# One layer of a decoder, DeltaNet branch and 32 experts: the projections from unsplit float32 in place of high and low parts

## The chip, the cores and the metric

The kernel runs on one core of a Trainium2 chip. The metric is the device time of one execution in microseconds (us), median over runs. The core has TensorE (PE in the profile, with its weight loads shown apart as PEld), VectorE (DVE), ScalarE (ACT), GpSimd (POOL), SyncE (SP, which issues most transfers here) and 16 DMA engines.

## The reference, cut to what matters

What is computed is a chain of blocks over 256 tokens of width 1024, all in float32: attention with its input and output projections, a convolutional feed-forward block, a block with a DeltaNet branch and a stick-breaking attention branch and gates, an output projection, and a mixture of 32 experts. The part that the change touches is the dense matrix products between activations and weights of the first four of these:

```python
qkv = jnp.einsum('bsd,de->bse', x, w_qkv)          # 1024 x 3072
return o @ w_o                                     # 1024 x 1024
u = _causal_dwconv(x @ w_up, conv_w, conv_b)       # 1024 x 5632
gate, up = jnp.split(u, 2, axis=-1)
return (jax.nn.silu(gate) * up) @ w_down           # 2816 x 1024
```

The block after it has an input projection of 22 pieces of 1024 x 256, two branch projections of 512 x 1024 and an output projection of 1024 x 1024 of the same kind. The experts' products aren't touched.

## The kernel before, in words

**Granules.** The projections' weights come from HBM in 79 pieces of 1 MB, here called granules: 12 for q, k and v (numbers 0 to 11), 4 for the attention's output (12 to 15), 33 for the feed-forward block (16 to 48, in steps of gate, up and down), 22 for the input projection (49 to 70), 4 for the two branches (71 to 74) and 4 for the output (75 to 78). SP loads granule n into slot n % 3 of `raw`, once granule n - 3 has been split (`load`, L629 to L633).

**The split.** The projections' operands are of TensorE's float32r type, and a float32 value is given to it as a high and a low part. ScalarE copies each granule into a float32r tile `whi` (`hi_part`, L849), and VectorE subtracts that from the granule to get the rest, `wlo` (`lo_part`, L1362). Both have two buffers, and a few granules (`own`) have tiles of their own. The activations are split in the same way: `hT_hi` and `hT_lo`, `oT_hi` and `oT_lo`, `hid_hi` and `hid_lo`, `osb_*`, `odn_*`. A product is then three matmuls, high by high, low by high and high by low, which is `split3`:

```python
pe.matmul(dst, lh, rh, start=start, stop=False, **kw)
pe.matmul(dst, lh, rl, start=False, stop=False, **kw)
return pe.matmul(dst, ll, rh, start=False, stop=stop, **kw)
```

**Counts.** A granule of the 64 with 1024 x 256 weights takes 16 calls of `split3` (8 slices of the depth by 2 tiles of 128 rows or features). 54 of them, and the 4 of the branches with 16 calls each, stream 256 columns a matmul (58 x 16 = 928 calls). In 10 granules of the input projection the 16 leading meta tokens are computed too, and a matmul streams 272 columns (160 calls). Each of the 11 feed-forward down granules takes 8 calls that stream 512 columns (88 calls). That is 1176 calls and 3528 float32r matmuls.

**Order.** All engines run a fixed order written by hand. In the attention, scores, transposes and products with the values of one pair of heads stand between the granules. The block with the DeltaNet branch follows `plan`, in which parts of granules stand between the many small products of the chain. After granule 74 SP begins to load the experts (`sp.wait_ge(s_gran, G_OUT)`), into a ring of six experts of three slots each. The experts' own matmuls (L2649, L2671) and those of the small chains are plain float32 before and after. `keep_warm` multiplies by the identity where TensorE would have nothing to do.

Of the kernel before, what the change touches and what calls it, by code (L numbers as in the profile page):

```python
# [7 lines left out]
F32 = mybir.dt.float32  # L8
# [10 lines left out]
P = 128  # L19
D = 1024  # L20
KD = D // P
# [66 lines left out]
def build(nc, a, out):  # L88
    with ExitStack() as ctx:
# [14 lines left out]
        def con(name, n=None, rows=P):  # L104
# [15 lines left out]
        OWN_SLOT = (14, 15, 48, 49)  # L120
# [7 lines left out]
        oT_hi = place("oT_hi", [P, KD, SEQ], PH + 49152, F32R)  # L128
        oT_lo = place("oT_lo", [P, KD, SEQ], PH + 57344, F32R)
# [3 lines left out]
        own = {n: (place(f"own_hi{n}", [P, GR], at, F32R), place(f"own_lo{n}", [P, GR], at + 8192, F32R))  # L133
               for n, at in zip(OWN_SLOT, (PH + 74752, PH + 24576, PH + 24576, PH + 49664))}
# [3 lines left out]
        hid_hi = place("hid_hi", [P, 2, 2, SEQ], PH + 83968, F32R)  # L138
        hid_lo = place("hid_lo", [P, 2, 2, SEQ], PH + 88064, F32R)
        MT = place("MT", [META, D], PH + 92160)  # L140
        ln_cols_rows = place("ln_cols_rows", [2 * KD, P], PH + 97280)
        h_cols = place("h_cols", [P, KD, NT], PH + 40960)
# [7 lines left out]
        def tiny(n):  # L150
# [18 lines left out]
        s_hi, s_lo, s_gran, s_ev = sem("s_hi"), sem("s_lo"), sem("s_gran"), sem("s_ev")  # L169
        s_ss, s_rt, s_dve, s_xn, s_xT, s_xhi, s_xlo = (sem(n) for n in ("s_ss", "s_rt", "s_dve", "s_xn", "s_xT", "s_xhi", "s_xlo"))  # L170
        s_S, s_mx, s_nmx, s_exp, s_prob, s_PT, s_probT, s_PV, s_oThi, s_oTlo = (
            sem(n) for n in ("s_S", "s_mx", "s_nmx", "s_exp", "s_prob", "s_PT", "s_probT", "s_PV", "s_oThi", "s_oTlo"))
        s_colsT, s_cols = sem("s_colsT"), sem("s_cols")
        s_gaff, s_gtap, s_gsilu, s_uaff, s_utap, s_hid, s_hidhi, s_hidlo = (
            sem(n) for n in ("s_gaff", "s_gtap", "s_gsilu", "s_uaff", "s_utap", "s_hid", "s_hidhi", "s_hidlo"))
        s_first_hi, s_first_lo = sem("s_first_hi"), sem("s_first_lo")
# [12 lines left out]
        assert OWN_SLOT == (G_WO + 2, G_WO + 3, G_IN - 1, G_IN)  # L189

        def hi_of(n):
            return own[n][0][:, :] if n in own else whi[:, n % H, :]

        def lo_of(n):
            return own[n][1][:, :] if n in own else wlo[:, n % H, :]
# [88 lines left out]
        plan_add("split", G_IN + 11)  # L284
# [95 lines left out]
        plan_add("split", G_BSB + 1)  # L380
# [3 lines left out]
        plan_add("odn")  # L384
# [54 lines left out]
        osb_hi = place("osb_hi", [P, 4, SEQ], PH + 58112, F32R)  # L439
        osb_lo = place("osb_lo", [P, 4, SEQ], PH + 62208, F32R)  # L440
        dE, dA, dN, dX, dT, dU = (place(n, [P, 2, DN_H, P], PH + 66304 + 4096 * i) for i, n in enumerate(("dE", "dA", "dN", "dX", "dT", "dU")))
        odn = place("odn", [P, DN_H, SEQ], PH + 66304 + 4 * 4096)
        odn_hi = place("odn_hi", [P, DN_H, SEQ], PH + 66304 + 4096, F32R)
        odn_lo = place("odn_lo", [P, DN_H, SEQ], PH + 66304 + 2 * 4096, F32R)
# [5 lines left out]
        mT = place("mT", [P, KD, SEQ], PH + 24576)  # L450
# [16 lines left out]
        def mat(ab, cc, c):  # L467
# [10 lines left out]
        s_A, s_N, s_qd, s_U, s_z, s_e, s_sp, s_cs, s_arg, s_w, s_pv, s_osbhi, s_osblo = (  # L478
            sem(n) for n in ("s_A", "s_N", "s_qd", "s_U", "s_z", "s_e", "s_sp", "s_cs", "s_arg", "s_w", "s_pv", "s_osbhi", "s_osblo"))
        s_sig, s_osq, s_on, s_odnhi, s_odnlo, s_m, s_mhi, s_mlo, s_lnrow = (  # L480
            sem(n) for n in ("s_sig", "s_osq", "s_on", "s_odnhi", "s_odnlo", "s_m", "s_mhi", "s_mlo", "s_lnrow"))
# [4 lines left out]
        def evacs(n):  # L486

            return 2 * (n + 1) if n < G_FFN else 2 * G_FFN + 2 * (n - G_IN + 1)
# [229 lines left out]
        def _(pool):  # L718
# [5 lines left out]
            pool.wait_ge(landed[0], 32)  # L724
# [7 lines left out]
            pool.wait_ge(landed[0], 48)  # L732
# [35 lines left out]
            pool.wait_ge(s_xlo, 13)  # L768
# [71 lines left out]
        def _(act):  # L840
# [20 lines left out]
            def norm_hi(q, tiles=range(TT), parts=range(2)):  # L861
                for t in tiles:
                    for f in parts:
                        act.wait_ge(s_xT, 4 * q + 2 * t + f + 1)
# [41 lines left out]
            def heads_hi(p):  # L906
                act.wait_ge(s_PV, p + 1)
                act.activation(oT_hi[:, p, :], PG[:, 2 + p % 2, 0:SEQ], ACT.Copy).then_inc(s_oThi, 1)
# [1903 lines left out]
```

## Time and profile before

| | |
|---|---|
| median of 3 runs | 842.64 us (842.39 to 843.23) |
| span of the profiled execution | 841.9 us |
| busy: PE, DVE, ACT | 821.3, 490.3, 378.3 us |
| weight loads of PE | 677.6 us |
| granted clock of TensorE, mean | 0.998 of 2.4 GHz |

The span is the profiled execution's own time, from its first to its last instruction. It is 0.7 us below the median of the runs. Busy time of PE counts a matmul from its start to its modelled end, and matmuls overlap, so what a matmul costs in a dense stretch is read from the distance between starts, not from its own length.

### The profile page before, as it was taken

The numbers are of one execution on the slowest core, as the hardware profiler recorded it, in microseconds if no ns is written. First come the engines' busy times: TensorE is split into PE (matmuls) and PEld (weight loads), VectorE is DVE, ScalarE is ACT, GpSimd is POOL, SyncE is SP. The second block draws the span as 40 slices with busy tenths as digits, with TensorE's granted clock in tenths as the row PEclk, the third lists the DMA queues.
The fourth block names the chain that finished last, engine by engine and source line by source line (L and its number), as shares of the span: only waits on it lengthen the run. The fifth ranks groups of instructions, "written<-read, shape, count | busy, mean of one in ns | idle before, by whom it ended". The sixth has DMA issues, their size and how long they took to land.

```text
span 841.9 us, 16143 instructions
## 1 busy us (share of the span) xinstructions
PE 821.3 (98%) x6626; PEld 677.6 (80%) x6626; DVE 490.3 (58%) x843; ACT 378.3 (45%) x573; POOL 57.6 (7%) x93
## 2 busy tenths in 40 slices
PE   6999999999999999999999999999999999999996
PEld 6999998999999998999988999999755555555542
DVE  4455667766766778867772445486763433333344
ACT  4556664554454467467444544664421111111123
POOL 0300032000000000200111000000110000010000
PEclk9999999999999999999999999999999999999999
DMA  8964462655555562644333332469989999999991
GB/s 284 298 214 130 137 172 90 200 180 171 196 190 178 180 208 93 200 140 142 120 102 101 102 102 81 171 217 412 357 329 409 409 409 409 409 408 409 409 401 62
DMA packets 102482, 194.35 MB, mean 231 GB/s; under 512 B 4669, under 2 KB 70560, under 8 KB 102288
## 3 DMA queue, kind: packets, MB, share of 16 engines
q1 hardware_dynamic: 99664, 185.61, 61.5%
q0 software_dynamic: 2176, 5.66, 2.1%
q10 hardware_dynamic: 576, 2.14, 0.7%
q8 instruction: 49, 0.80, 0.4%
q14 instruction: 17, 0.14, 0.0%
HBM read 192.34 MB, written 1.05 MB: 230 GB/s over the span
## 4 chain that ended last, share of the span: by engine, by line
PE 89%; DVE 4%; DMA 3%; ACT 2%; issue 1%; SPq 0%; ACTq 0%; DVEq 0%
PE PG L2046 15%; PE PG L2048 14%; PE PG L2047 14%; PE PG L2649 13%; PE PG L2671 6%; PE PM L2680 3%; PE PM L2046 3%; PE PM L2048 3%; PE PM L2047 3%; DMA expert_w<-in_expert_w_up 2%; PE PM L2502 1%; PE PG L2658 1%; ACT whi L849 1%; PE PG L2113 1%; PE PM L2127 1%
## 5 line engine op out<-in xcount | busy, mean ns | idle before, releaser
L2046 PE MATMUL PG<-hT_hi,whi 128*128 128x256 f32 (+1 forms) x816 | 235.5, 289 | 0.0
L2048 PE MATMUL PG<-hT_hi,wlo 128*128 128x256 f32 (+1 forms) x816 | 230.5, 282 | 0.0
L2047 PE MATMUL PG<-hT_lo,whi 128*128 128x256 f32 (+1 forms) x816 | 230.3, 282 | 0.0
L1362 DVE TENSOR_TENSOR wlo<-raw,whi 128x2048 fp32r<-128x2048 f32 x73 | 167.2, 2290 | 66.8 <-ACT whi L849 66.7
L2046 PEld LDWEIGHTS PG<-hT_hi,whi 128*128 128x128 f32 x816 | 153.9, 189 | 6.1 <-issue 2.9
L2048 PEld LDWEIGHTS PG<-hT_hi,wlo 128*128 128x128 f32 x816 | 154.1, 189 | 0.0
L2047 PEld LDWEIGHTS PG<-hT_lo,whi 128*128 128x128 f32 x816 | 153.6, 188 | 0.2
L849 ACT ACTIVATE whi<-raw 128x2048 fp32r<-128x2048 f32 x73 | 139.4, 1910 | 22.4 <-PE PG L2048 20.1
L2649 PE MATMUL PG<-expert_w,xw 128*64 128x256 f32 x992 | 114.1, 382 | 1.9 <-DMA expert_w<-in_expert_w_up 1.9
L2649 PEld LDWEIGHTS PG<-expert_w,xw 128*64 128x64 f32 x992 | 68.7, 137 | 38.6 <-issue 6.7
L2671 PE MATMUL PG<-expert_w,hid 128*64 128x512 f32 x256 | 61.2, 599 | 0.1
L1957 DVE SCALAR_TENSOR_TENSOR y_lo<-PG,small,y_hi 128x512 fp32r<-128x512 f32 x16 | 12.0, 750 | 76.0 <-ACT y_hi L1281 76.0
L1275 ACT ACTIVATE gusum<-PG 128x256 f32<-128x256 f32 x32 | 12.3, 385 | 96.8 <-PE PG L2649 96.8
L2671 PEld LDWEIGHTS PG<-expert_w,hid 128*64 128x64 f32 x256 | 17.0, 136 | 26.6 <-issue 24.4
L2046 PE MATMUL PG<-whi,hT_hi 128*128 128x256 f32 x128 | 36.8, 288 | 1.3 <-DVE wlo L1362 1.2
L1957 DVE SCALAR_TENSOR_TENSOR y_in_pad<-PG,small,y_in_pad 128x512 fp32r<-128x512 f32 x15 | 11.3, 750 | 44.3 <-ACT y_in_pad L1281 44.3
L2048 PE MATMUL PG<-whi,hT_lo 128*128 128x256 f32 x128 | 36.0, 281 | 0.0
L1281 ACT ACTIVATE y_hi<-PG,small 128x512 fp32r<-128x512 f32 x16 | 11.0, 688 | 55.5 <-PE PG L2671 55.5
L2047 PE MATMUL PG<-wlo,hT_hi 128*128 128x256 f32 x128 | 35.9, 281 | 0.0
L815 POOL COPY xw<-pair 128x512 f32 x31 | 19.2, 619 | 195.5 <-PE PG L2649 178.1
L2046 PE MATMUL PM<-whi,hid_hi 128*128 128x512 f32 x80 | 31.7, 396 | 0.2 <-DVE wlo L1362 0.2
L2048 PE MATMUL PM<-whi,hid_lo 128*128 128x512 f32 x80 | 31.3, 391 | 0.0
(527 smaller groups left out, 1356.9 us busy)
## 6 DMA issues: line engine op xcount, KB each, us to landing
expert_w<-in_expert_w_gate SPq DMA_DIRECT2D x64, 512.0 KB, 15.5
expert_w<-in_expert_w_up SPq DMA_DIRECT2D x64, 512.0 KB, 15.8
expert_w<-in_expert_w_down SPq DMA_DIRECT2D x32, 1024.0 KB, 16.9
raw<-in_ffn_w_up SPq DMA_DIRECT2D x22, 1024.0 KB, 5.1
raw<-in_w_in SPq DMA_DIRECT2D x22, 1024.0 KB, 5.2
raw<-in_moba_w_qkv SPq DMA_DIRECT2D x12, 1024.0 KB, 5.6
raw<-in_ffn_w_down SPq DMA_DIRECT2D x11, 1024.0 KB, 4.9
raw<-in_moba_w_o SPq DMA_DIRECT2D x4, 1024.0 KB, 5.1
```

What stands on the lines that cost most here:

```text
L815: pool.tensor_copy(xw[i2][:, :, :], pair[:, :, bass.ds(at, WIN)]).then_inc(s_win, 1)
L849: act.activation(hi_of(n), raw[:, n % R, :], ACT.Copy).then_inc(s_hi, 1)
L1275: act.activation(gusum[i2][:, :], PG[:, i2, 0:EFF], ACT.Copy).then_inc(s_gu, 1)
L1281: act.activation(y, src, ACT.Copy, scale=slotw[i2]).then_inc(s_yhi, 1)
L1362: dve.tensor_tensor(lo_of(n), raw[:, n % R, :], hi_of(n).bitcast(F32), ALU.subtract).then_inc(s_lo, 1)
L1957: dve.scalar_tensor_tensor(y[1], src, slotw[i2], y[0].bitcast(F32), ALU.mult, ALU.subtract).then_inc(s_y, 1)
L2046: pe.matmul(dst, lh, rh, start=start, stop=False, **kw)
L2047: pe.matmul(dst, lh, rl, start=False, stop=False, **kw)
L2048: return pe.matmul(dst, ll, rh, start=False, stop=stop, **kw)
L2649: mm = pe.matmul(PG[WIN * h:WIN * h + WIN, i2, 0:EFF], x[:, KH * kind + k, :], w[:, h, k, :], start=kind + k == 0, stop=kind == 1 and k == ...
L2671: mm = pe.matmul(result[WIN * h:WIN * h + WIN, :], hid2[i2][:, f, :], w[:, f, 512 * h:512 * h + 512], start=f == 0, stop=f == 1)
L2680: mm = pe.matmul(PM[:, 2 * t + h, :], hot[x, P * t:P * t + P], y[x], start=first and n == 0, stop=last and n == 1)
```

## The change

The high and low parts are gone. `raw` has six slots instead of three, and SP loads a granule once TensorE has done with the one six before it. TensorE multiplies the float32 granule from `raw` by the float32 activation, with one matmul where `split3` made three. It waits for the landing of the granule (`arrived`) and for one evacuation of each activation, instead of for the low parts. The rest of the diff follows from this: tiles that held parts are gone, `h_cols` is `hT` itself, the counter of evacuations `s_ev` is cut into one for each engine and stage, granule 0 comes as two halves, and one expert load is issued a little earlier.

```diff
-        hT_hi = place("hT_hi", [P, KD, NT], 29440, F32R)
-        hT_lo = place("hT_lo", [P, KD, NT], 38144, F32R)
-
-        R, H = 3, 2
+        hT = place("hT", [P, KD, NT], 29440)
+
+        R = 6
         raw = place("raw", [P, R, GR], 46848)
-        whi = place("whi", [P, H, GR], 71424, F32R)
-        wlo = place("wlo", [P, H, GR], 87808, F32R)
...
+        def arrived(eng, n, it=0):
+
+            if n == 0:
+                eng.wait_ge(s_half0, 16)
+            eng.wait_ge(landed[n % R], 16 * (n // R + 1) + 16 * (6 // R) * it)
...
                 if n >= R:
-                    sp.wait_ge(s_lo, n - R + 1 + 6 * it)
+                    sp.wait_ge(s_gran, n - R + 1 + 6 * it)
...
-            sp.wait_ge(s_mlo, 4)
-            for e, kind in ((3, 0), (3, 1), (2, 2), (4, 0), (4, 1)):
+            sp.wait_ge(s_m, 4)
+            for e, kind in ((3, 0), (3, 1), (2, 2), (4, 0), (4, 1), (3, 2)):
                 expert_load(e, kind, e)
             sp.wait_ge(s_gran, G_END)
-            expert_load(3, 2, 3)
...
-            def hi_part(n, it=0):
-                act.wait_ge(landed[n % R], 16 * (n // R + 1) + 32 * it)
-                if n >= H and n not in own:
-                    before = max(m for m in range(n) if m % H == n % H and m not in own)
-                    act.wait_ge(s_gran, before + 1 + 6 * it)
-                act.activation(hi_of(n), raw[:, n % R, :], ACT.Copy).then_inc(s_hi, 1)
...
-            def lo_part(n, it=0):
-                dve.wait_ge(s_hi, n + 1 + 6 * it)
-                dve.tensor_tensor(lo_of(n), raw[:, n % R, :], hi_of(n).bitcast(F32), ALU.subtract).then_inc(s_lo, 1)
...
-            def split3(dst, lh, ll, rh, rl, start, stop, **kw):
-
-                pe.matmul(dst, lh, rh, start=start, stop=False, **kw)
-                pe.matmul(dst, lh, rl, start=False, stop=False, **kw)
-                return pe.matmul(dst, ll, rh, start=False, stop=stop, **kw)
...
-                        mm = split3(PG[:, bank + f, 0:c.stop - c.start], hw[:, k, P * f:P * f + P], lw[:, k, P * f:P * f + P],
-                                    ah[:, k, c], al[:, k, c], k == 0, k == KD - 1)
+                        mm = pe.matmul(PG[:, bank + f, 0:c.stop - c.start], w[:, k, P * f:P * f + P], x[:, k, c], start=k == 0, stop=k == KD - 1)
...
-                            mm = split3(PM[:, 2 * t + f, :], hid_hi[:, par, c, x], hid_lo[:, par, c, x], hw[:, c, w], lw[:, c, w],
-                                        False, True, skip_group_check=True)
+                            mm = pe.matmul(PM[:, 2 * t + f, :], hid[:, par, c, x], wd[:, c, w], start=False, stop=True, skip_group_check=True)
```

**TensorE, feed-forward loop.** Before, the last call of an up granule and the first of the down granule behind it:

```order
L2046 MATMUL PG<-hT_hi,whi 128x256
L2047 MATMUL PG<-hT_lo,whi 128x256
L2048 MATMUL PG<-hT_hi,wlo 128x256
L2222 REGISTER_ALU
L2046 MATMUL PM<-whi,hid_hi 128x512
L2047 MATMUL PM<-wlo,hid_hi 128x512
L2048 MATMUL PM<-whi,hid_lo 128x512
```

After, the two halves of the loop's body, a gate and an up granule of 16 matmuls each ahead of a down granule of 8:

```order
L1913 MATMUL PG<-hT,raw 128x256 x32
L2074 MATMUL PM<-raw,hid 128x512 x8
L2081 ISA
L1913 MATMUL PG<-hT,raw 128x256 x32
L2074 MATMUL PM<-raw,hid 128x512 x8
```

Each three rows have become one, in the same places.

**TensorE, input projection.** Before, one call of granule 56, the column sums of squares of the DeltaNet branch (`sqb` by ones, plain float32, two matmuls in the program), and the granule's next matmul:

```order
L2046 MATMUL PG<-hT_hi,whi 128x272
L2047 MATMUL PG<-hT_lo,whi 128x272
L2048 MATMUL PG<-hT_hi,wlo 128x272
L2416 MATMUL PM<-sqb,cst 128x272 x2
L2046 MATMUL PG<-hT_hi,whi 128x272
```

After:

```order
L2270 MATMUL PM<-small,cst 16x4
L1913 MATMUL PG<-hT,raw 128x272 x56
L2252 MATMUL PM<-sqb,cst 128x272 x2
L1913 MATMUL PG<-hT,raw 128x272 x8
L2252 MATMUL PM<-sqb,cst 128x272 x2
```

The small products stand where they stood between the same granules.

**VectorE, from the second branch granules to the first rows of the output projection.** Before (`gT` are the gates, `mT` the mixed branches that the output projection reads, `X` the residual):

```order
L1362 TENSOR_TENSOR wlo<-raw,whi 128x2048
L1650 TENSOR_TENSOR hT_lo<-mT,hT_hi 128x2x256 x2
L1642 TENSOR_TENSOR gT<-PG,gT 128x512
L1644 TENSOR_TENSOR mT<-mT,gT 128x512
L1642 TENSOR_TENSOR gT<-PG,gT 128x512
L1644 TENSOR_TENSOR mT<-mT,gT 128x512
L1650 TENSOR_TENSOR hT_lo<-mT,hT_hi 128x2x256 x2
L1362 TENSOR_TENSOR wlo<-raw,whi 128x2048
L1654 SCALAR_TENSOR_TENSOR X<-X,PG 128x2x256
```

After:

```order
L1515 TENSOR_TENSOR gT<-PG,gT 128x512
L1517 TENSOR_TENSOR mT<-mT,gT 128x512
L1515 TENSOR_TENSOR gT<-PG,gT 128x512
L1517 TENSOR_TENSOR mT<-mT,gT 128x512
L1521 SCALAR_TENSOR_TENSOR X<-X,PG 128x2x256
```

The low parts of `mT` and of the granules are gone, and nothing has come in their place.

## Rows read from the trace of the kernel before

**Rows 1.** The page: part 1, TensorE; part 2, its granted clock in 40 slices.

```profile
PE 821.3 (98%) x6626; PEld 677.6 (80%) x6626; DVE 490.3 (58%) x843; ACT 378.3 (45%) x573; POOL 57.6 (7%) x93
...
PEclk9999999999999999999999999999999999999999
```

**Rows 2.** Waits of PE: who waited for whom, us in total, times, longest.

```profile
PE PG L2649 <- DMA expert_w<-in_expert_w_up: 1.9, 2, 1.4
PE PG L2046 <- DVE wlo L1362: 1.2, 1, 1.2
...
PE PM L2046 <- DVE hid_lo L1499: 0.3, 1, 0.3
PE PM L2046 <- DVE wlo L1362: 0.2, 1, 0.2
```

**Rows 3.** Busy time of each engine in the feed-forward loop, 158 to 314 us.

```profile
158.00:314.00 156.00, 155.84 (x1093) 144.86 (x1094) 109.39 (x122) 81.93 (x85) 0.00 (x0) 1.00 0.57 185
```

**Rows 4.** The largest group of PE by form: xcount, busy us, mean ns.

```profile
L2046 PE MATMUL PG<-hT_hi,whi 128*128 128x256 f32 x656 | 187.8, 286 | 0.0
```

**Rows 5.** PE in order of time: first and last matmul of three dense stretches (start, length).

```profile
135.06 0.36 PE L2046 MATMUL PG<-hT_hi,whi 128*128 128x256 f32 x1
...
146.33 0.28 PE L2048 MATMUL PG<-hT_hi,wlo 128*128 128x256 f32 x1
...
363.05 0.38 PE L2046 MATMUL PG<-hT_hi,whi 128*128 128x272 f32 x1
...
384.20 0.29 PE L2048 MATMUL PG<-hT_hi,wlo 128*128 128x272 f32 x1
...
277.18 0.43 PE L2046 MATMUL PM<-whi,hid_hi 128*128 128x512 f32 x1
...
282.48 0.39 PE L2048 MATMUL PM<-whi,hid_lo 128*128 128x512 f32 x1
```

**Rows 6.** Plain float32 on PE, in order of time; then by line: length min, median, max.

```profile
12.87 3.78 PE L2113 MATMUL PG<-cst 128*128 128x128 f32 x22
...
129.73 2.74 PE L2209 MATMUL PM<-X,cst 128*128 128x512 f32 x6
...
384.33 1.08 PE L2416 MATMUL PM<-sqb,cst 128*128 128x272 f32 x4
...
606.06 3.67 PE L2649 MATMUL PG<-expert_w,pair 128*64 128x256 f32 x32
...
L2209 PE MATMUL PM<-X,cst x8: 590/592/595, 129.7 to 134.5; 128*128 128x512 f32 x8
...
L2416 PEld LDWEIGHTS PM<-sqb,cst x16: 188/189/190, 384.2 to 396.2; 128*128 128x128 f32 x16
L2416 PE MATMUL PM<-sqb,cst x16: 391/392/393, 384.3 to 396.4; 128*128 128x272 f32 x16
```

**Rows 7.** PE in order of time at its two longest waits for a split.

```profile
316.37 0.39 PE L2048 MATMUL PM<-whi,hid_lo 128*128 128x512 f32 x1
317.05 0.50 PE L2046 MATMUL PM<-own_hi,hid_hi 128*128 128x512 f32 x1 [0.28 <-DVE hid_lo L1499]
...
567.22 0.28 PE L2048 MATMUL PG<-whi,hT_lo 128*128 128x256 f32 x1
568.67 0.35 PE L2046 MATMUL PG<-whi,hT_hi 128*128 128x256 f32 x1 [1.17 <-DVE wlo L1362]
```

**Rows 8.** Loads of granules: size, median us to landing; the page's group of the subtractions.

```profile
raw<-in_ffn_w_up SPq DMA_DIRECT2D x22, 1024.0 KB, 5.1
...
L1362 DVE TENSOR_TENSOR wlo<-raw,whi 128x2048 fp32r<-128x2048 f32 x73 | 167.2, 2290 | 66.8 <-ACT whi L849 66.7
```

**Rows 9.** First issue of an expert load; the last expert's gate and up matmuls.

```profile
561.32 0.34 SPq L677 DMA_DIRECT2D expert_w<-in_expert_w_gate  x1
...
815.92 1.95 PE L2649 MATMUL PG<-expert_w,xw 128*64 128x256 f32 x16 [1.40 <-DMA expert_w<-in_expert_w_up]
818.40 1.95 PE L2649 MATMUL PG<-expert_w,xw 128*64 128x256 f32 x16 [0.54 <-DMA expert_w<-in_expert_w_up]
```

More of the change, by code:

```diff
@@ L1485, in taps, with ffn_step @@
                             ins.then_inc(s_tap, 1)
[L1487 removed]
+            def ffn_step(n, j, par, it):
                 taps(cgate, par, 0, 2 * j, s_gaff, s_gtap, j)
[L1489 to L1491 removed]
                 taps(cup, par, 2, FT + 2 * j, s_uaff, s_utap, j)
[L1493 to L1494 removed]
                 dve.wait_ge(s_gsilu, j + 1)
@@ L1590, in _ @@
                     shifted_rows(st[1])
-                elif kind == "part":
-                    if st[2] + st[3] == 0 and st[1] not in (G_IN, G_IN + 10):
-                        lo_part(st[1] + 1)
-                elif kind == "split":
-                    lo_part(st[1])
                 elif kind == "out":
@@ L2075, in tokens, with features_half @@
                         for k in range(k0, k1):
-                            c = slice(P * t, P * t + P)
-                            mm = split3(PG[:, bank + t, 0:256], ah[:, k, c], al[:, k, c], hw[:, k, :], lw[:, k, :], k == 0, k == KD - 1)
-                        if t == 0 and first is not None:
-                            mm.then_inc(first, 1)
+                            mm = pe.matmul(PG[:, bank + t, 0:256], x[:, k, P * t:P * t + P], w[:, k, :], start=k == 0, stop=k == KD - 1)
                 mm.then_inc(s_gran, 1)
-            def features_half(n, bank, ah, al, f):
-                hw, lw = w_of(n)
-                if n + f > 0:
-                    pe.wait_ge(s_lo, n + 1)
+            def features_half(n, bank, x, f):
+                w = w_of(n)
+                if n > 0:
+                    arrived(pe, n)
@@ L2096, in features_half, with tokens_part @@
+                        pe.wait_ge(s_xcv, TT)
+                    mm = pe.matmul(PG[:, bank, SEQ * f:SEQ * f + SEQ], w[:, k, P * f:P * f + P], x[:, k, 0:SEQ], start=k == 0, stop=k == KD - 1)
                 if f == 1:
                     mm.then_inc(s_gran, 1)
-            def tokens_part(n, bank, ah, al, t, k0, k1, banks=PG):
-                pe.wait_ge(s_lo, n + 1)
-                hw, lw = w_of(n)
-                c = slice(P * t, P * t + P)
+            def tokens_part(n, bank, x, t, k0, k1, banks=PG):
+                arrived(pe, n)
+                w = w_of(n)
@@ L2104, in tokens_part @@
                 for k in range(k0, k1):
-                    mm = split3(banks[:, bank, 256 * t:256 * t + 256], ah[:, k, c], al[:, k, c], hw[:, k, :], lw[:, k, :],
-                                k == 0 and t == 0, k == KD - 1, skip_group_check=True)
+                    mm = pe.matmul(banks[:, bank, 256 * t:256 * t + 256], x[:, k, P * t:P * t + P], w[:, k, :],
+                                   start=k == 0 and t == 0, stop=k == KD - 1, skip_group_check=True)
                 if t == TT - 1 and k1 == KD:
@@ L2293, in branch @@
                     for k in range(4):
-                        x = slice(P * f, P * f + P)
-                        mm = split3(dst, hw[:, k, x], lw[:, k, x], ah[:, k, :], al[:, k, :], k == 0, k == 3)
+                        mm = pe.matmul(dst, w[:, k, P * f:P * f + P], a[:, k, :], start=k == 0, stop=k == 3)
                     if n >= G_BDN and f == 1:
@@ L2300, in rows_of_tile @@
             def rows_of_tile(n, bank, t, k0, k1):
-                pe.wait_ge(s_lo, n + 1)
-                hw, lw = w_of(n)
-                c = slice(P * t, P * t + P)
+                arrived(pe, n)
+                w = w_of(n)
                 for k in range(k0, k1):
-                    mm = split3(PG[:, bank + t, 0:256], hT_hi[:, k, c], hT_lo[:, k, c], hw[:, k, :], lw[:, k, :], k == 0, k == KD - 1)
+                    mm = pe.matmul(PG[:, bank + t, 0:256], mT[:, k, P * t:P * t + P], w[:, k, :], start=k == 0, stop=k == KD - 1)
                 return mm
```

398 lines of the change are left out of this document (132 added, 266 removed).

## The prediction

> **What bounds the kernel now.** I read the page first. TensorE is busy for 98% of the span and its clock is granted in full in every slice [rows 1], so the next question is whether that busy time is dense work or waiting in disguise. The list of its waits says dense: from the splits it waited 1.2 us once and 0.5 us in two more places, and for the experts' weights 1.9 us [rows 2]. In the feed-forward loop the windows show PE busy for 155.84 of 156.00 us, while VectorE works 109 us and ScalarE 82 us of it [rows 3]. So up to the experts the end moves with the number of TensorE's passes and with their price, and the split work of the other two engines lies beside it.
>
> The busy time of one matmul misleads here: the mean is 286 ns [rows 4], but starts in a dense stretch are much closer. That distance is the price, and the next step was to find it for both kinds of matmul.
>
> **The price of a split call.** From 135.06 to 146.33 us stand the gate and up granules of the first step, 2 x 16 calls of three matmuls, so 96 matmuls and 95 distances: 11.27 / 95 = 0.1186 us, 0.356 us a call [rows 5]. From 363.05 to 384.20 us stand 56 calls of 272 columns, 167 distances: 0.1267, 0.380 a call. A down granule from 277.18 to 282.48 us, 24 matmuls of 512 columns, 23 distances: 0.2304, 0.691 a call.
>
> **The price of a plain float32 matmul.** This is where one can go wrong by a factor of two. `keep_warm(11, ...)` issues 11 matmuls, and the trace has x22 records of it. The program's order has two matmuls of L2416 at 384.33 us, and the trace has x4 [rows 6]. So a plain float32 matmul stands in the trace as two records, a float32r one as one. Per record of 512 columns (L2209): (2.74 - 0.592) / 5 = 0.4296 us. Per record of 272 columns (L2416): (1.08 - 0.391) / 3 = 0.2297 us. The two give 0.00083 us for a column, and so 0.2164 us for a record of 256. A matmul is two records: 0.433 us for 256 columns, 0.459 for 272, 0.859 for 512. The first isn't in the trace on the whole array, so I bound it. From below: half of 512 columns' price, 0.430. From above: the experts' matmuls of 256 columns fill half the array, two run side by side, and 32 records take 3.67 us, so (3.67 - 0.39) / 15 = 0.219 a pair of records, 0.437 a matmul [rows 6] (0.39 is taken from L2416's length as that of the last). I take 0.433, since L2416 is the same use of the array with nearly the same columns.
>
> **The sum.**
> - 928 calls of 256 columns: 928 x (0.433 - 0.356) = +71.3 us.
> - 160 calls of 272: 160 x (0.459 - 0.380) = +12.7 us.
> - 88 calls of 512: 88 x (0.859 - 0.691) = +14.8 us.
> - Waits for splits that go: 317.05 - 316.37 less a distance of 0.23 is 0.45, and 568.67 - 567.22 less 0.12 is 1.33 [rows 7]; the wait of 0.2 in the list and what lies below its sight I put at 0.5. Together -2.3 us.
> - What the split cost the other engines (73 whole subtractions on VectorE alone, 2.29 us each [rows 8], a copy on ScalarE ahead of each, and the activations' parts): nothing comes back, since it lay beside TensorE's work [rows 3]. Uncovered, each granule would pay its 2.29 us; the waits in [rows 2] say that it was covered in all but three places.
> - The start: the first projection follows `keep_warm`, which runs from 12.87 us and is unchanged [rows 6]. Operands that are ready earlier wait for it. 0.
> - The loads: a granule lands 5.1 us after its issue [rows 8]. SP now waits for TensorE and not for the split, and the slot is free only when the granule has been used up, but six slots mean five granules of 16 x 0.433 = 6.9 us ahead of need. The landing is hidden by some 29 us; uncovered it would cost up to 5.1 us a granule. 0.
> - The small chains between the granules (softmax, DeltaNet levels): each gets a longer TensorE stretch to hide under than before, and VectorE and ScalarE have fewer instructions queued in front of it. 0.
> - The experts: their first load is issued at 561.32 us, when granule 74 is done, and their first matmul starts at 606.06 us [rows 6, 9]. Of the sum above 64 calls x 0.077 = 4.9 us, less the 1.33 and a little, lie between the two. Loads and matmuls then run nearly level: the last expert waited 1.40 and 0.54 us for its weights [rows 9]. The ring is full before the first matmul in either kernel, so loads shift with the matmuls. If they shift less, those 1.9 us go: 0 to -1.9, and I take 0.
>
> That makes +98.8 - 2.3 = +96.5, and 841.9 + 96.5 = 938.4 us of span. The runs' median lies 0.7 us above the span of the profiled execution, so 939.
>
> **A rule that speaks against this.** The weight loads are busy 677.6 us, 80% of the span [rows 1], and 144.86 of 156 us in the feed-forward loop [rows 3]. The change takes three weight loads a call down to two. The Trainium skill, "Perfetto Trace Analysis", section Identifying the Most-Contended Engine, says to judge TensorE's headroom by the busy share of its weight loads and not by that of its matmuls. By that reading the calls would get cheaper by a third, and the sum would be -151 us; by the distances it is +96.5. The trace decides for the distances: L2416 has a weight load of 0.188 us for each record [rows 6] and still spaces its records by its columns.
>
> **Rivals.**
> - *Weight loads set the pace.* Three loads are 93% busy in the loop [rows 3], so a call would cost two thirds. All split calls now take 928 x 0.356 + 160 x 0.380 + 88 x 0.691 = 452 us; a third is 151, and 842.6 - 151 - 2 = 690 us. It decides if a record of 256 columns costs a load's share (0.119) and not its columns. Against it: 0.2297 and 0.4296 us a record grow with the columns. The same time would come out if a plain matmul were one record on the chip and I misread the doubling. Faster; chance 0.03.
> - *A pass costs what a float32r pass costs.* Two records at about twice the columns' price look like four passes. The Trainium skill, "FP8 and Floating Point Precision", section TensorE Precision Notes, gives four passes for true FP32. If each cost 0.1186, a call would cost four thirds of now, and the time would be 842.6 + 151 - 2 = 991 us. Against it: 272 columns would be 4 x 0.1267 = 0.507, and L2416 shows 0.459. Chance 0.04.
> - *A new wait takes some of it:* a granule's landing behind expert or row loads, or the clock falling to 1.2 GHz in a stretch of plain float32. The clock is full in all slices, also those of the experts, which are plain float32 [rows 1]. 951 to 985 us; chance 0.03.
> - *No change,* by gains and losses that happen to meet: nothing in the rows makes it. 0.01.
>
> **How the numbers follow.** The forecast has 0.89. Its price of 256 columns is bounded by 0.430 and 0.437 (-3 to +4 us over 928 calls); the first matmul after a change of form is longer than the others by 0.08 us (0.36 against 0.28 in [rows 5]), and as much at each of 79 granules, paid before and not after or the other way round, is 6 us either way. So 931 to 950 us holds the forecast's own cases nearly all and leaves out the rivals' 0.11. Slower by over 0.2% (about what a measurement of this kernel can tell from no change): 0.89 + 0.04 + 0.03 = 0.96. Within it 0.01. Faster 0.03.
>
> **What would show it.** In the profile after, a projection's matmul stands as two records, 0.216 us apart for 256 columns: a gate or up granule takes 6.9 us instead of 5.7, a feed-forward step 20.7 instead of 16.9. VectorE's busy time falls by at least the 73 subtractions' 167 us, and SP's waits are on TensorE. The first expert matmul starts near 702 us, and from there to the end the profile looks as before. The prediction is wrong if records of 256 columns are spaced by other than 0.215 to 0.219 us, if TensorE has waits of over 3 us in all for landings or evacuations before the experts, or if the stretch from the first expert matmul to the end isn't 236 us.

## The result and the profile after

The changed kernel takes **936.62 us** (median of 4 runs, 935.7 to 937.01), the kernel before, on the same chip, 842.59 us (842.39 to 843.23). The ratio is 1.1113, 95% interval 1.1097 to 1.1128: slower by 11.1%, or 94 us. The span of its profiled execution is 934.7 us.

The page of the kernel after, busy time and the granted clock in 40 slices, answers to [rows 1] and to the table of before:

```profile
PE 916.2 (98%) x5450; PEld 680.5 (73%) x5450; DVE 295.3 (32%) x732; ACT 220.1 (24%) x458; POOL 57.8 (6%) x93
...
PEclk9999999999999999999999999999999999999999
```

TensorE is as full as before, at a full clock, 93 us longer. VectorE has lost 195 us of work and ScalarE 158 us, and the kernel is no faster for it.

PE in order of time, after (start, length, line, tiles, count; records that follow each other on one line are drawn together, and a row at the edge of the stretch asked for counts only those inside it):

```profile
15.65 0.81 PE L1942 MATMUL PG<-hT,raw 128*128 128x256 f32 x3
...
148.32 1.45 PE L2054 MATMUL PM<-X,cst 128*128 128x512 f32 x3
...
201.38 7.03 PE L2074 MATMUL PM<-raw,hid 128*128 128x512 f32 x16
208.24 13.98 PE L1913 MATMUL PG<-hT,raw 128*128 128x256 f32 x64
222.06 7.03 PE L2074 MATMUL PM<-raw,hid 128*128 128x512 f32 x16
...
380.64 0.66 PE L2102 MATMUL PG<-cst,MT 16*128 16x16 f32 x8
...
452.50 3.83 PE L1913 MATMUL PG<-hT,raw 128*128 128x272 f32 x16
...
699.11 0.87 PE L2485 MATMUL PG<-expert_w,pair 128*64 128x256 f32 x6
```

The 32 matmuls of a gate and an up granule stand as x64 records, and the 8 of a down granule as x16. From 208.24 to 222.06 us is 13.82 / 64 = 0.2159 us a record of 256 columns. From 201.38 to 208.24 is 6.86 / 16 = 0.429 for 512. The 16 records of 272 columns take 3.83 us with the last one's 0.39, so (3.83 - 0.39) / 15 = 0.229. A feed-forward step, from one down granule to the next, takes 222.06 - 201.38 = 20.68 us.

The same view of the kernel before, at the two landmarks that [rows 6] lacks:

```profile
16.41 0.36 PE L2046 MATMUL PG<-hT_hi,whi 128*128 128x256 f32 x1
...
322.71 0.67 PE L2258 MATMUL PG<-cst,MT 16*128 16x16 f32 x8
```

The four landmarks are the first matmul of the first projection, of the feed-forward block's norm (`X,cst`, 129.73 before in [rows 6]), of the meta tokens' (`MT`) and of the experts (606.06 in [rows 6]). The differences of their starts give where the time went:

| stretch | before, us | after, us | difference |
|---|---|---|---|
| start to first projection | 16.41 | 15.65 | -0.8 |
| attention (256 calls of 256 columns) | 113.32 | 132.67 | +19.4 |
| feed-forward (352 of 256, 88 of 512) | 192.98 | 232.32 | +39.3 |
| from there to the experts (320 of 256, 160 of 272) | 283.35 | 318.47 | +35.1 |
| experts to the end | 235.84 | 235.59 | -0.2 |
| span | 841.9 | 934.7 | +92.8 |

Waits of PE after, which answer to [rows 2]:

```profile
PE PM L1898 <- DVE XN L1294: 2.1, 1, 2.1
PE PG L2485 <- DMA expert_w<-in_expert_w_up: 2.0, 2, 1.3
...
```

The waits on `wlo` and `hid_lo` are gone from the list, whose shortest entry is 0.2 us. No projection waits for a landing: L1913, L1942, L1951, L2039, L2074 and L2147 aren't in the list.

### The profile page after: what moved, and what is told of

It is laid out like the page before. It is cut to its first block, busy times and chain, and to the rows that moved or that the text cites. A ratio compares the mean times of both kernels' runs of the same rounds, so it can differ in the third digit from the quotient of the medians.

```text
span 934.7 us, 13451 instructions
## 1 busy us (share of the span) xinstructions
PE 916.2 (98%) x5450; PEld 680.5 (73%) x5450; DVE 295.3 (32%) x732; ACT 220.1 (24%) x458; POOL 57.8 (6%) x93
## 3 DMA queue, kind: packets, MB, share of 16 engines
q0 software_dynamic: 2176, 5.66, 1.8%
## 4 chain that ended last, share of the span: by engine, by line
PE 94%; DMA 3%; DVE 2%; SPq 0%; issue 0%; ACT 0%; DVEq 0%; ACTq 0%
PE PG L1913 34%; PE PG L2485 11%; PE PM L2074 8%; PE PG L1942 6%; PE PG L2507 6%; PE PG L1951 5%; PE PM L2516 3%; PE PG L2138 2%; DMA expert_w<-in_expert_w_up 2%; PE PG L2147 1%; PE PG L1927 1%; PE PM L2338 1%; PE PG L2494 1%; PE PG L2039 1%; PE PM L2138 1%; PE PM L1973 1%
## 5 line engine op out<-in xcount | busy, mean ns | idle before, releaser
L1913 PE MATMUL PG<-hT,raw 128*128 128x256 f32 (+1 forms) x1408 | 319.0, 384 | 0.0
L1913 PEld LDWEIGHTS PG<-hT,raw 128*128 128x128 f32 x1408 | 264.6, 190 | 44.3 <-issue 5.0
L2074 PE MATMUL PM<-raw,hid 128*128 128x512 f32 x176 | 77.2, 592 | 0.0
L2074 PEld LDWEIGHTS PM<-raw,hid 128*128 128x128 f32 x176 | 33.4, 190 | 37.8 <-issue 37.3
L1942 PE MATMUL PG<-hT,raw 128*128 128x256 f32 x256 | 57.0, 381 | 0.0
L1387 DVE SCALAR_TENSOR_TENSOR cgate<-PG,cols,cgate 128x255 f32<-128x255 f32 (+1 forms) x44 | 19.9, 480 | 111.0 <-ACT cgate L934 109.0
L1942 PEld LDWEIGHTS PG<-hT,raw 128*128 128x128 f32 x256 | 48.1, 190 | 7.8 <-issue 1.5
L934 ACT ACTIVATE cgate<-PG,cols 128x256 f32<-128x256 f32 x22 | 11.2, 561 | 128.9 <-PE PG L1913 128.9
L1387 DVE SCALAR_TENSOR_TENSOR cup<-PG,cols,cup 128x255 f32<-128x255 f32 (+1 forms) x44 | 19.9, 480 | 54.7 <-ACT cup L934 53.5
L1951 PE MATMUL PG<-raw,hT 128*128 128x256 f32 x128 | 28.6, 381 | 0.0
L1795 DVE SCALAR_TENSOR_TENSOR hits<-place_row,slot_at,share_row 128x256 f32<-128x256 f32 x64 | 28.0, 479 | 0.0
L1951 PEld LDWEIGHTS PG<-raw,hT 128*128 128x128 f32 x128 | 24.1, 190 | 4.0 <-issue 0.8
L1815 DVE SCALAR_TENSOR_TENSOR y_in_pad<-PG,small,y_in_pad 128x512 fp32r<-128x512 f32 x15 | 11.3, 750 | 45.0 <-ACT y_in_pad L1207 45.0
## 6 DMA issues: line engine op xcount, KB each, us to landing
raw<-in_moba_w_qkv SPq DMA_DIRECT2D x11, 1024.0 KB, 11.1
```

What stands on the lines that cost most here:

```text
L1387: ins = dve.scalar_tensor_tensor(dst[:, par, f, back:SEQ], PG[:, bank + f, 0:SEQ - back], col((2 - back) * 2 * FT + tile0 + f), dst[:, par ...
L1795: dve.scalar_tensor_tensor(hits[:, n, :], place1_row[:, n, :], mine, share_row[:, n, :], ALU.is_equal, ALU.mult).then_inc(s_parts, 1)
L1815: dve.scalar_tensor_tensor(y[1], src, slotw[i2], y[0].bitcast(F32), ALU.mult, ALU.subtract).then_inc(s_y, 1)
L1913: mm = pe.matmul(PG[:, bank + f, 0:c.stop - c.start], w[:, k, P * f:P * f + P], x[:, k, c], start=k == 0, stop=k == KD - 1)
L1942: mm = pe.matmul(PG[:, bank, SEQ * f:SEQ * f + SEQ], w[:, k, P * f:P * f + P], x[:, k, 0:SEQ], start=k == 0, stop=k == KD - 1)
L1951: mm = pe.matmul(banks[:, bank, 256 * t:256 * t + 256], x[:, k, P * t:P * t + P], w[:, k, :], start=k == 0 and t == 0, stop=k == KD - 1, s ...
```

## The experiments

**The price by itself.** A kernel without the layer runs 48 matmuls each of several forms, one group behind the other, on one weight tile `W` of plain float32 and its float32r copy `Wr`. The core of it:

```diff
+            for i in range(N):
+                pe.matmul(PG[:, 0, 0:256], W[:, i % 8, :], A[:, 0:256], start=i == 0, stop=i == N - 1, skip_group_check=True)
...
+            for i in range(N):
+                pe.matmul(PG[:, 0, 0:256], Wr[:, i % 8, :], Ar[:, 0:256], start=i == 0, stop=i == N - 1, skip_group_check=True)
```

> No layer is computed here and the output is zeros: TensorE alone runs blocks of 48 matmuls each, plain float32 and float32r, of 128, 192, 256, 384 and 512 columns, with new weights in each matmul, and for 256 columns also with the same weights, with four banks in turn, and with each weights twice. My theory (a plain float32 matmul is two records, each at about two clock periods a column, and loads are hidden): distance of records 0.162 us for 192, 0.216 for 256, 0.323 for 384, 0.429 for 512; 128 columns at about 0.112, where the load may show. Same weights change nothing. For float32r 0.119 for 256, 0.173 for 384, 0.227 for 512 us. Rival (loads set the pace): 128, 192 and 256 columns of a form cost the same, and the same weights twice cost no less only if the load is still issued. Rival (a pass costs what a float32r pass costs): a record of 256 costs 0.237 us. Open: whether the 12 ns that a float32r matmul of 256 columns takes beyond its columns are its load (then 128 and 192 columns cost 0.119 too) or a fixed sum for each matmul (then 192 costs 0.092).

PE in order of time:

```profile
19.29 10.88 PE L134 MATMUL PG<-A,W 128*128 128x128 f32 x96
30.01 15.77 PE L136 MATMUL PG<-A,W 128*128 128x192 f32 x96
45.61 20.88 PE L138 MATMUL PG<-A,W 128*128 128x256 f32 x96
...
97.29 41.36 PE L142 MATMUL PG<-A,W 128*128 128x512 f32 x96
138.49 20.88 PE L144 MATMUL PG<-A,W 128*128 128x256 f32 x96
159.02 5.66 PE L146 MATMUL PG<-Ar,Wr 128*128 128x128 f32 x48
164.52 5.55 PE L148 MATMUL PG<-Ar,Wr 128*128 128x192 f32 x48
169.91 5.94 PE L150 MATMUL PG<-Ar,Wr 128*128 128x256 f32 x48
...
184.01 11.08 PE L154 MATMUL PG<-Ar,Wr 128*128 128x512 f32 x48
194.93 5.92 PE L156 MATMUL PG<-Ar,Wr 128*128 128x256 f32 x48
```

48 plain matmuls stand as x96 records, 48 of float32r as x48. Less the length of the last record (mean by form: 0.379, 0.592, 0.283 and 0.390 us), a record of 256 columns costs (20.88 - 0.379) / 95 = 0.2158 us and one of 512 (41.36 - 0.592) / 95 = 0.4292, so a plain matmul 0.432 and 0.858. One of float32r costs (5.94 - 0.283) / 47 = 0.1204 and (11.08 - 0.390) / 47 = 0.2274. L144 and L156 use one weight tile throughout and cost the same, but the profile has as many weight loads for them (96 and 48), so this says nothing about what a load costs. For plain float32 the rival of the loads falls, since 128, 192 and 256 columns cost 0.1116, 0.1626 ((15.77 - 0.326) / 95) and 0.2158 us a record. For float32r its sign is half there: 128 and 192 columns cost 0.1145 and 0.1123 us, and only above that does the price grow with the columns. In all, a plain matmul replaces 3.6 (256 columns) to 3.8 (512) float32r passes, where the split needs three.

**The price alone, in the kernel.** The kernel before with one plain float32 matmul on the high parts; the splits, their order and the ring of three slots stay. The low parts are left out of the products.

```diff
-                pe.matmul(dst, lh, rh, start=start, stop=False, **kw)
-                pe.matmul(dst, lh, rl, start=False, stop=False, **kw)
-                return pe.matmul(dst, ll, rh, start=False, stop=stop, **kw)
+                return pe.matmul(dst, lh.bitcast(F32), rh.bitcast(F32), start=start, stop=stop, **kw)
```

> The kernel before with the three matmuls of a split call replaced by one plain float32 matmul of the two high parts (the low parts are computed but not used, so their share of each product is left out). All split work of ScalarE and VectorE, the ring of three and all waits stay. It prices the passes alone. My theory: 928 x (0.432 - 0.356) + 160 x (0.459 - 0.380) + 88 x (0.858 - 0.691) = +97.8 us, and of the 2 us of waits for splits most go because TensorE gives the split more time: 938 to 941 us, 1 to 4 us above the changed kernel. Rival (the split work is what the other engines' contention or waits cost, and the change's loss is smaller or larger by it): below 930 or above 945 us.

It took 936.63 us (936.05 to 937.23), ratio 1.111 (1.1092 to 1.1129). That is the changed kernel's time, within the 1.5 us or so that the intervals leave open, and it lies 1.4 us under the range expected. Its page says what ran beside it:

```profile
PE 916.3 (98%) x5450; PEld 680.3 (73%) x5450; DVE 490.5 (52%) x843; ACT 379.6 (41%) x573; POOL 57.1 (6%) x93
```

VectorE and ScalarE have the split work of before (490.5 and 379.6 us), and it costs nothing that can be told. The change's loss is the price of its passes.

**One kind of granule alone.** Only the 11 down granules take the plain matmul, on the high parts; the low parts are left out there.

```diff
-                            mm = split3(PM[:, 2 * t + f, :], hid_hi[:, par, c, x], hid_lo[:, par, c, x], hw[:, c, w], lw[:, c, w],
-                                        False, True, skip_group_check=True)
+                            mm = pe.matmul(PM[:, 2 * t + f, :], hid_hi[:, par, c, x].bitcast(F32), hw[:, c, w].bitcast(F32),
+                                           start=False, stop=True, skip_group_check=True)
```

> The kernel before with the 88 split calls of 512 columns (the feed-forward down granules) replaced by one plain float32 matmul of the high parts each (their low parts' share is left out); all else as before. My theory: 88 x (0.858 - 0.691) = +14.7 us, 857 us; the waits of 0.2 and 0.45 us for the low parts of the activation may stay. Rival (plain float32 of 512 columns costs four float32r passes): 88 x (0.922 - 0.691) = +20 us, 863 us.

856.06 us (855.58 to 856.59), ratio 1.0155 (1.0139 to 1.017): +13.1 us against the 842.94 measured beside it, with an interval of +11.7 to +14.3, where the term says +14.8. The feed-forward block alone grew by 13.6 us, from 193.0 to 206.6 (335.5 - 128.9), and the wait of 0.3 us for `hid_lo` is gone from its list. The rival of four float32r passes, +20 us, is out; where the last us under the term went isn't shown.

**The ring.** The changed kernel with three slots, and with two:

```diff
-        R = 6
-        raw = place("raw", [P, R, GR], 46848)
+        R = 2
+        raw = place("raw", [P, R, GR], 71424)
```

> The changed kernel with a ring of three granules in place of six. My theory: a granule takes TensorE 6.9 us and lands 5.1 us after its issue, so two granules ahead are 13.8 us and cover it: within 0.5 us of the changed kernel, 936 to 937.5 us. Rival (the depth of the ring carries part of the result, since a slot is now free only when the granule has been used up): 2 to 10 us slower than the changed kernel.

> The changed kernel with a ring of two granules (placed 24 KB higher). One granule ahead is 6.9 us against a landing of 5.1 us plus issue: my theory is that it is just covered where matmuls are dense and the granule stands alone, and shows where rows or constants load beside it and in the down granules: 937 to 945 us. Rival (a landing takes longer when the next load is issued only after use, and each of 79 granules pays 1 us or more): over 990 us.

Three slots: 936.15 us (935.95 to 938.89), ratio 1.1116 (1.1101 to 1.1131), the same as six, with one landing in the list (`raw<-in_moba_w_o`, 0.4 us). Two slots: 950.41 us (949.66 to 956.23), ratio 1.1296 (1.1266 to 1.1327), and the expectation was too low. The waits of PE with two slots:

```profile
PE PG L2039 <- DMA raw<-in_moba_w_o: 4.2, 1, 4.2
PE PG L2485 <- DMA expert_w<-in_expert_w_up: 2.4, 5, 0.7
PE PG L2507 <- DMA expert_w<-in_expert_w_down: 2.1, 2, 1.7
...
PE PG L1942 <- DMA raw<-in_moba_w_qkv: 2.0, 1, 2.0
PE PG L2147 <- DMA raw<-in_w_out: 1.9, 1, 1.9
```

Landings are waited for at three single places (4.2, 2.0, 1.9 us), and the experts' weights cost 2.4 + 2.1 us of waiting where they cost 2.0 after. That is 10.6 of the 13.8 us. By the four landmarks 8.1 us were lost ahead of the feed-forward block, none in it, 2.4 us between it and the experts and 3.0 us behind; some 2 us of the first part are in no wait of the list. In the feed-forward loop one granule of 6.9 us hides the landing of 5.1 us, and no wait stands there. Six slots buy nothing over three.

**Fewer passes on the split.** Two runs were meant to bound the other side: what if a call cost two passes, or one? Two of three leaves the product high by low out of each call, one of three leaves out both products with a low part. All splits are still made.

```diff
                 pe.matmul(dst, lh, rh, start=start, stop=False, **kw)
-                pe.matmul(dst, lh, rl, start=False, stop=False, **kw)
-                return pe.matmul(dst, ll, rh, start=False, stop=stop, **kw)
+                return pe.matmul(dst, lh, rl, start=False, stop=stop, **kw)
```

> The kernel before with the low by high matmul left out of each split call (that part of each product is left out); all split work stays. If TensorE's passes alone set the time up to the experts: 928 x 0.119 + 160 x 0.127 + 88 x 0.230 = 151 us less, 692 us. My theory adds that VectorE with 109 us busy in the 156 us of the feed-forward loop is the next bound there: TensorE would need 104 us, VectorE 109 or somewhat more, so 5 to 15 us of the gain are lost there and some in the DeltaNet chain: 695 to 712 us. Rival (weight loads set the pace): the same 692 and no engine near its bound.

> The kernel before with only the high by high matmul of each split call (both parts with a low factor are left out); all split work stays. By TensorE's passes alone 842.6 - 301 = 541 us. My theory: what the split work costs when it isn't covered shows here. Feed-forward loop at VectorE's 109 us or more in place of 52, and each granule elsewhere pays a subtraction of 2.29 us and a copy of 1.91 us beside the chain's own work: 600 to 660 us, with VectorE busy over 80% in the feed-forward loop. Rival (the split work is nearly free even uncovered): under 570 us.

Two of three took 774.63 us (773.0 to 776.33), ratio 0.9183 (0.9167 to 0.9198), one of three 763.7 us (760.76 to 764.15), ratio 0.9048 (0.9028 to 0.9068). Both miss: of 151 us that the first pass taken away was worth by the distances, 68 came, and of the second 11. One step of the feed-forward loop of one of three, DVE in order of time and then PE (the last row of PE is cut by the edge):

```profile
182.66 0.68 DVE L1497 TENSOR_TENSOR hid<-cgate,cup 128x512 f32<-128x512 f32 x1
184.04 0.69 DVE L1499 TENSOR_TENSOR hid_lo<-hid,hid_hi 128x512 fp32r<-128x512 f32 x1 [0.70 <-ACT hid_hi L975]
185.84 2.29 DVE L1362 TENSOR_TENSOR wlo<-raw,whi 128x2048 fp32r<-128x2048 f32 x1 [1.11 <-ACT whi L849]
188.05 1.88 DVE L1481 SCALAR_TENSOR_TENSOR cgate<-PG,cols,cgate 128x255 f32<-128x255 f32 x4
189.84 2.29 DVE L1362 TENSOR_TENSOR wlo<-raw,whi 128x2048 fp32r<-128x2048 f32 x1
192.04 1.89 DVE L1481 SCALAR_TENSOR_TENSOR cup<-PG,cols,cup 128x255 f32<-128x255 f32 x4
193.84 2.28 DVE L1362 TENSOR_TENSOR wlo<-raw,whi 128x2048 fp32r<-128x2048 f32 x1
196.04 0.68 DVE L1497 TENSOR_TENSOR hid<-cgate,cup 128x512 f32<-128x512 f32 x1
...
182.79 3.79 PE L2046 MATMUL PG<-hT_hi,whi 128*128 128x256 f32 x16 [1.01 <-DVE wlo L1362]
188.18 2.15 PE L2046 MATMUL PG<-hT_hi,whi 128*128 128x256 f32 x16 [1.60 <-DVE wlo L1362]
192.18 2.77 PE L2046 MATMUL PM<-whi,hid_hi 128*128 128x512 f32 x8 [1.85 <-DVE wlo L1362]
196.18 1.22 PE L2046 MATMUL PG<-hT_hi,whi 128*128 128x256 f32 x4 [1.23 <-DVE wlo L1362]
```

The step takes 196.04 - 182.66 = 13.38 us. VectorE waits twice for ScalarE in it, 1.8 us together, and works for the other 11.6 us (its rows overlap by some 0.1 us, so they add up to more). Three subtractions are 6.9 us of it. TensorE works for 8.7 us and waits 4.7 us for `wlo`: VectorE has become the bound, together with what it waits for on ScalarE.

With two of three the step takes 202.99 - 188.13 = 14.86 us, where 16.9 x 2/3 = 11.3 is TensorE's own time. DVE there, its start, its four waits and the next start:

```profile
188.13 0.68 DVE L1497 TENSOR_TENSOR hid<-cgate,cup 128x512 f32<-128x512 f32 x1
189.51 0.69 DVE L1499 TENSOR_TENSOR hid_lo<-hid,hid_hi 128x512 fp32r<-128x512 f32 x1 [0.70 <-ACT hid_hi L975]
191.32 2.29 DVE L1362 TENSOR_TENSOR wlo<-raw,whi 128x2048 fp32r<-128x2048 f32 x1 [1.11 <-ACT whi L849]
...
198.63 1.96 DVE L1481 SCALAR_TENSOR_TENSOR cup<-PG,cols,cup 128x255 f32<-128x255 f32 x4 [0.89 <-ACT cup L958]
200.78 2.29 DVE L1362 TENSOR_TENSOR wlo<-raw,whi 128x2048 fp32r<-128x2048 f32 x1 [0.19 <-ACT whi L849]
202.99 0.69 DVE L1497 TENSOR_TENSOR hid<-cgate,cup 128x512 f32<-128x512 f32 x1
```

Its work is 12.0 us and its waits for ScalarE are 2.9 us: together they are the step. In the wait for `cup` ScalarE itself had waited for TensorE, in the others for VectorE's `hid` or its own queue.

**Is it the subtraction, or only the last link?** TensorE waits on `wlo`, but `wlo` itself waits on ScalarE's copy. Three kernels take the subtraction's length away and keep its place and its semaphores. The one with two passes takes the product high by high twice.

```diff
-                dve.tensor_tensor(lo_of(n), raw[:, n % R, :], hi_of(n).bitcast(F32), ALU.subtract).then_inc(s_lo, 1)
+                dve.tensor_tensor(lo_of(n)[:, 0:8], raw[:, n % R, 0:8], hi_of(n)[:, 0:8].bitcast(F32), ALU.subtract).then_inc(s_lo, 1)
```

> The kernel before with two float32r matmuls a call, both high by high, so the same number of passes as in the run with two of three (774.63 us), but with VectorE's subtractions of the low parts cut down to 8 columns each (the granules, and the activations likewise, or to a fourth). ScalarE's copies stay. The low parts are left out of every product, and the high product counts twice. Theory A: the run with two of three came out 80 us above TensorE's own time because TensorE waited there for the 73 granule subtractions (35.2 + 5.6 us of waits on wlo in the list) and for what they delayed behind them on VectorE. Then the time falls to 700 to 725 us, and wlo is gone from the waits. Theory B: ScalarE's copies, or the slots of the ring, set the pace there, and the subtraction is only the last link: then the waits move to whi or to a landing, and the time stays at 755 to 775 us.

> The kernel before with one float32r matmul a call, high by high, and the subtractions of the granules (73 of 2.29 us, and the few in halves) cut down to 8 columns; the activations' subtractions stay. The low parts are left out of every product. Against the run with one of three (763.7 us, waits on wlo 59.9 + 18.8 us). Theory A, the subtraction is the bound there: 670 to 700 us. Theory B, ScalarE's copies or landings are: 740 to 765 us, with the waits moved to whi or to raw.

> As the run before, but the subtractions of the activations' low parts are cut down as well. The low parts are left out of every product. Its waits on them in the run with one of three were hT_lo 5.0 + 0.2 and hid_lo 3.5 us. Theory A: 5 to 15 us below the run with the granules' subtractions alone cut down, so 655 to 695 us. Theory B (VectorE had nothing to do with it): the same as that run within 2 us. In both, TensorE's own time of one pass a call, 842.6 - 2 x 151 = 541 us, isn't reached, since the small chains no longer have a projection to lie beside.

| passes a call | all subtractions | granules' cut down | activations' too |
|---|---|---|---|
| two | 774.63 us | | 715.87 us |
| one | 763.7 us | 687.08 us | 686.67 us |

Two passes: 715.87 us (714.91 to 716.76), ratio 0.849 (0.8476 to 0.8504). One pass: 687.08 us (685.58 to 689.24), ratio 0.8155 (0.8134 to 0.8176), and 686.67 us (684.79 to 693.4), ratio 0.8167 (0.8118 to 0.8215). For the granules the first theory holds: both times lie in its ranges. Their subtractions alone cost 76.6 us at one pass, 0.97 us for each of the 79 granules. At two passes all subtractions together cost 58.8 us. For the activations at one pass the second theory is the one that came: the run is within 0.4 us of the one before it, and the 5 to 15 us expected didn't come. The wait list at two passes without subtractions, where two of three had 35.2 us in 28 waits for `wlo`:

```profile
PE PG L2048 <- DVE wlo L1362: 2.2, 3, 1.5
```

At one pass with the granules' subtractions cut down, 42.1 us of waits for `wlo` stayed, where one of three had 78.7. The list has 10.8 us of them for `PM` and this row:

```profile
PE PG L2048 <- DVE wlo L1362: 31.3, 23, 2.2
```

There the subtraction is the last link, behind ScalarE's copy. ACT in order of time, one step of the loop, in the run with the granules' subtractions cut down:

```profile
181.69 1.01 ACT L958 ACTIVATE cup<-PG,cols 128x256 f32<-128x256 f32 x2
182.58 1.92 ACT L849 ACTIVATE whi<-raw 128x2048 fp32r<-128x2048 f32 x1
185.44 0.63 ACT L975 ACTIVATE hid_hi<-hid 128x512 fp32r<-128x512 f32 x1 [0.94 <-DVE hid L1498]
185.98 1.90 ACT L849 ACTIVATE whi<-raw 128x2048 fp32r<-128x2048 f32 x1
187.78 1.00 ACT L958 ACTIVATE cgate<-PG,cols 128x256 f32<-128x256 f32 x2
188.68 1.91 ACT L849 ACTIVATE whi<-raw 128x2048 fp32r<-128x2048 f32 x1
190.48 0.62 ACT L966 ACTIVATE cgate<-cgate 128x512 f32<-128x512 f32 x1
191.00 1.01 ACT L958 ACTIVATE cup<-PG,cols 128x256 f32<-128x256 f32 x2
```

ScalarE works for 8.4 us of a step of 191.00 - 181.69 = 9.3 us and waits once, 0.94 us, for VectorE's `hid`. So with the subtractions gone ScalarE's copies and evacuations, with that one wait, are the step.

The landmarks of the stages put a place to it. What the distances alone would give is an estimate: the stage before, less 0.119, 0.127 and 0.230 us for each call of 256, 272 and 512 columns and each pass taken away.

| us | to the feed-forward block | in it | from there to the experts | from the experts on |
|---|---|---|---|---|
| two passes, by distances | 99.3 | 130.9 | 225.0 | 235.8 |
| two of three | 113.9 | 169.7 | 255.1 | 235.9 |
| two, all subtractions cut down | 108.6 | 132.0 | 238.6 | 235.7 |
| one pass, by distances | 68.8 | 68.8 | 166.6 | 235.8 |
| one of three | 111.0 | 159.1 | 256.3 | 235.9 |
| one, granules' subtractions cut down | 105.4 | 113.9 | 230.4 | 235.6 |

At two passes the subtractions are all that the feed-forward block lost: without them it comes within 1.1 us of TensorE's own time. The 23 us that stay lost at two passes, and most of what is lost at one, lie in the stages with the small chains. How much of that is the chains, ScalarE's copies or the clock no run here tells apart.

These three kernels are faster than both that are compared here, but they leave out the low parts of every product; none of the runs that keeps them beats the kernel before.

## Why the prediction was right

**The price of a pass** carried it. Plain float32 stands in the trace as two records a matmul, and both sizes follow the columns. 0.2159 us a record of 256 columns was predicted as 0.2164, 0.429 of 512 as 0.4296, and 0.229 of 272 as 0.2297. With these the three terms come to 928 x (0.432 - 0.356) + 160 x (0.458 - 0.380) + 88 x (0.858 - 0.691) = 70.5 + 12.5 + 14.7 = +97.7 us, against 98.8. The run with the price alone leaves room for nothing else above some 1.5 us.

**Waits that go** were -2.3 us. The three stages with projections grew by 93.8 us, 3.9 less than 97.7. Of these, 2.1 are in the feed-forward block (352 x 0.076 + 14.7 = 41.4 against 39.3) and 1.7 behind it (320 x 0.076 + 12.5 = 36.8 against 35.1), where the named waits of 0.45 and 1.33 stood. What is over the 2.3 can lie in waits below the list's sight, in the prices' last digit, or in the profiled execution of before (see the next paragraph); no run tells these apart.

**The start** was put at 0 and is -0.8 us. With the prices (-1.1), the waits (-1.6) and the experts (-0.2) that makes the span 3.7 us shorter than the 938.4 forecast; the median lies 1.9 us above the span where 0.7 was taken, and so 939 is 2.4 us above 936.62. In every other execution on record the time is 1.7 to 2.1 us above its own span. So the profiled execution of before, with its span of 841.9 us, took some 1.2 us more than the median one, and 0.7 was no property of the kernel. That is why the spans differ by 92.8 us and the medians by 94.0. Between the medians +96.5 us was forecast, so 2.5 us too much; of the 3.7 us by which the span is short, 1.2 say nothing of the change.

**The other engines' work** was put at 0, with its cover named: TensorE's three passes. That is right for this change (936.62 with the splits gone, 936.63 with them kept). The note on what lies uncovered was off twice. There are 77 whole subtractions and 4 halves, since 4 stand under `own_lo` and not under `wlo`. And a granule's subtraction cost 0.97 us at one pass and not 2.29: in the loop a step lost 13.38 - 9.31 = 4.1 us of its 6.9, because without them ScalarE's copies held the pace.

**The loads** were put at 0 with 29 us to spare. Three slots give the same time as six with one landing of 0.4 us seen, and with two slots landings cost 8.1 us in three places. SP's longest waits are on TensorE, as was said.

**The experts** start at 699.11 us, where about 702 was predicted, and the stretch behind is 235.6 us, where 236 was. VectorE's busy time fell by 195 us, where at least 167 was said.

**The rivals.** *Weight loads set the pace* (690 us) fell with the distances. Behind it stood the rule of the Trainium skill, "Perfetto Trace Analysis", section Identifying the Most-Contended Engine, to read headroom from the weight loads' busy share (it names the share of peak arithmetic beside it). Here that share of the loads fell from 80% to 73% while the kernel became 11% slower, so the trace disagrees. The run with two of three would have been 692 us by TensorE's passes alone and took 774.63, and 715.87 with the subtractions cut down. So a third off TensorE's time doesn't by itself give 690 us; how near to it a kernel without the split work would come isn't shown. *A pass costs what a float32r pass costs* (991 us) fell with the price: 0.432 us is 3.6 matmuls of 0.1204, not 4. The four passes that the Trainium skill, "FP8 and Floating Point Precision", section TensorE Precision Notes, gives for true FP32 do agree with the trace, if a pass is taken at float32r's price of its columns alone: 4 x 256 x (0.2274 - 0.1204) / 256 = 0.428 us. *A new wait* isn't in the list.

**What I got wrong** were the expectations of two of three and one of three. The first did read that VectorE had 109 of 156 us in the loop [rows 3] and TensorE would keep 104, and allowed 5 to 15 us for it. The feed-forward block alone lost 38.8 us (169.7 against 130.9). What it left out were VectorE's waits for ScalarE, 2.9 us a step: the engines hand each other `whi`, `hid_hi` and the evacuations in a fixed order, so a step is VectorE's work and these waits together, 14.86 us and not 12. Outside the block another 44.7 us went, where "some" was expected. One of three was expected too low in the same way. VectorE is busy for 84.57 of the 100 us from 120 to 220 us, as was said. But the feed-forward block lost 90.3 us where 57 were expected, and the two stages beside it lost 132 us against the distances, where the range left at most 62 (660 - 541 - 57).

## What to carry to other kernels

Price a change of number format by the distance between records in a dense stretch, and count records against the program's matmuls first: a plain float32 matmul took two records and the time of 3.6 to 3.8 float32r passes, so splitting into three float32r products pays as long as its copies and subtractions lie beside the matmuls. It also needs wide matmuls. By the prices measured here three float32r passes of 256 columns cost 0.361 us against 0.432 for the plain one, but at 192 columns 0.337 against 0.325 and at 128 columns 0.344 against 0.223: there the plain matmul is the cheaper one. That holds for the run of the prices; in a kernel it wasn't tried. Work that is hidden is free only up to its margin; before a pass is taken off the bounding engine, set the busy time that will be left to it beside that of the next engine in the same window, and add that engine's waits for its own partners in each step: here 12.0 us of work took 14.9. Taking away hidden work (195 and 158 us of it here) buys nothing.

## What the runs showed of the hardware

A float32r matmul isn't simply half a record of plain float32. Records of plain float32 with 128, 256 and 512 columns cost 0.1116, 0.2158 and 0.4292 us ((10.88 - 0.275) / 95 for the first), so almost in proportion, with some 0.003 us fixed. Float32r matmuls of 256 and 512 columns cost 0.1204 and 0.2274 us, with 0.013 us fixed, but below 256 columns the price soon stops falling: (5.55 - 0.273) / 47 = 0.1123 us at 192 and (5.66 - 0.278) / 47 = 0.1145 us at 128. The price of 192 lies between the expectation's two answers, 0.092 (a fixed sum) and 0.119 (the load), nearer to the second. What sets this floor no run here shows. A plain matmul of 128 columns, two records, then costs 0.223 us, less than two of float32r.

TensorE's granted clock was 0.998 on the mean before, without gaps to speak of, and 0.873 in one of three, which had many. The granted clock in two stretches of the step shown above, of one of three:

```profile
182.80:186.50 3.70, 3.70 (x16) 3.48 (x16) 1.90 (x3) 2.43 (x2) 0.00 (x0) 0.50 0.76 257
188.20:190.20 2.00, 2.00 (x16) 1.93 (x16) 1.86 (x5) 1.70 (x2) 0.00 (x0) 1.00 0.30 65
```

The same sixteen matmuls take 3.79 us at 0.50 (1.2 GHz) and 2.15 us at 1.00 (2.4 GHz). Ahead of each TensorE had waited, 1.01 and 1.60 us, so the wait just before doesn't tell which level comes. With the granules' subtractions cut down it is 0.944, so a part of the 76.6 us may be the clock's and not the wait's. In the step shown it isn't: both of VectorE's waits are for copies that ScalarE made behind `hid`, and TensorE's speed enters neither. For the other stages no run here tells.
